# Moving three of the eight largest cache copies from layer 0 to layer 1, in 1 MB pieces on GpSimd's queue, and the delta rule's input loads from the first norm's block to the next one

## The reference

```python
# layer 0: convolution module beside a gated delta rule
z = h @ w_in                                   # 1024 -> 3080 columns
... depthwise convolutions, layer norm, SiLU, l2 norms ...
od, s_new = _gated_delta(q, k, v, g, beta, s0) # recurrent matrices, new state returned
x = x + mixed @ w_out
x = _tail(x, ...)                              # PEER: 8 heads x 16 gathered experts, then a gated embedding
# layer 1: attention with three (window, dilation) groups, then the same kind of tail
outs, caches = _mixer_dilated_sample(h, pos, caches, w_in, w_out)
```

```python
kv_all = jnp.concatenate([cache, kv_new], axis=1)
keep = min(win, L + T)
bufs.append(kv_all[:, L + T - keep:])
```

## Time and profile before

| | |
|---|---|
| time, median of 3 runs | 2553.03 us (2549.06 to 2556.84) |
| profiled execution: its own time | 2553.16 us |
| its span, first to last instruction | 2551.4 us |
| PE busy | 2052.6 us (80%) |
| DVE busy | 1281.3 us (50%) |
| ACT busy | 778.3 us (31%) |
| POOL busy | 644.4 us (25%) |
| moved by DMA | 874.97 MB, mean 343 GB/s |
| mean granted TensorE clock | 0.914 |

### The profile page before, as it was taken

How to read it: one execution, slowest core, us unless ns; L and a number is a source line. 1 busy time by engine, 2 the same in 40 slices (tenths; PEclk the granted TensorE clock), 3 DMA queues, 4 the chain that set the end, 5 groups by cost and what they waited for, 6 DMA issues and landing times. The chain is left out here.

```text
span 2551.4 us, 25632 instructions
## 1 busy us (share of the span) xinstructions
PE 2052.6 (80%) x9026; PEld 1023.6 (40%) x9026; DVE 1281.3 (50%) x3157; ACT 778.3 (31%) x2275; POOL 644.4 (25%) x645
## 2 busy tenths in 40 slices
PE   5975796478887898877689999987887887988766
PEld 4764684253222243322244565454532222432222
DVE  0076653164776667765511031123556677666754
ACT  0143100023444344443411121121234444344443
POOL 0000000024443444434201000000344444454341
PEclk8987775789999999999789999999899999999978
DMA  6794999669999999999938755753899999999995
GB/s 208 265 336 155 330 329 339 246 263 392 427 427 427 427 427 411 427 427 427 421 151 321 273 206 205 286 206 124 326 427 427 427 427 427 427 425 427 427 427 246
DMA packets 129427, 874.97 MB, mean 343 GB/s; under 512 B 15876, under 2 KB 29700, under 8 KB 45195
## 3 DMA queue, kind: packets, MB, share of 16 engines
q0 software_dynamic: 92160, 662.74, 62.5%
q1 hardware_dynamic: 37139, 210.60, 23.3%
HBM read 861.98 MB, written 118.81 MB: 384 GB/s over the span
## 5 line engine op out<-in xcount | busy, mean ns | idle before, releaser
L1433 PE MATMUL tail_acc<-tail_ring,tail_diag 128*128 128x512 f32 x1216 | 596.8, 621 | 113.1 <-ACT tail_diag L1292 111.9
L1180 DVE CUSTOM_DVE_ANT_0 tail_ring<-tail_ring,all_h 128x1024 f32<-128x1024 f32 x344 | 418.7, 1222 | 239.8 <-DMA tail_ring<-in_peer_uv,tail_idx 239.3
L1573 POOL DMA_INDIRECT mid_wring<-in_peer_uv,tail_idx x232 | 239.1, 1031 | 1005.8 <-DVE all_x L1065 528.7
L1433 PE MATMUL tail_acc<-mid_wring,tail_diag 128*128 128x512 f32 x832 | 413.3, 624 | 98.7 <-ACT tail_diag L1292 98.4
L1573 POOL DMA_INDIRECT tail_ring<-in_peer_uv,tail_idx x344 | 368.7, 1072 | 478.6 <-PE tail_acc L1433 412.8
L1433 PEld LDWEIGHTS tail_acc<-tail_ring,tail_diag 128*128 128x128 f32 x1216 | 216.4, 192 | 478.3 <-ACT tail_diag L1292 298.1
L1180 DVE CUSTOM_DVE_ANT_0 mid_wring<-mid_wring,all_h 128x1024 f32<-128x1024 f32 x232 | 283.3, 1223 | 175.0 <-DMA mid_wring<-in_peer_uv,tail_idx 173.5
L1286 ACT ACTIVATE tail_gelus<-tail_dots 128x1 f32<-128x1 f32 x576 | 116.2, 202 | 723.7 <-DVE tail_dots L1180 723.5
L1433 PEld LDWEIGHTS tail_acc<-mid_wring,tail_diag 128*128 128x128 f32 x832 | 147.8, 193 | 352.9 <-ACT tail_diag L1292 223.0
L1684 PE MATMUL mix_acc<-mid_wring,all_hT 128*128 128x512 f32 x576 | 273.2, 609 | 1.5 <-PEq L80 1.4
L1292 ACT ACTIVATE tail_diag<-all_ident,tail_weights 128x128 f32<-128x128 f32 x512 | 205.5, 401 | 26.8 <-PE tail_acc L1433 9.9
(11 more groups left out here) (363 smaller groups left out, 2083.3 us busy)
## 6 DMA issues: line engine op xcount, KB each, us to landing
mid_wring<-in_w_qkv SPq DMA_DIRECT2D x18, 2048.0 KB, 8.5
out_kv_s<-in_cache_kv_w SPq DMA_DIRECT2D x8, 4064.0 KB, 49.5
mix_ring<-in_kT POOLq DMA_DIRECT2D x16, 1024.0 KB
mix_ring<-in_v_rows POOLq DMA_DIRECT2D x16, 1024.0 KB
ab_ring_w<-in_w_in_ab SPq DMA_DIRECT2D x6, 2048.0 KB, 11.1
mix_ring<-in_kT POOLq DMA_DIRECT2D x16, 768.0 KB, 9.2
mix_ring<-in_v_rows POOLq DMA_DIRECT2D x16, 768.0 KB, 9.2
mid_wring<-in_w_out SPq DMA_DIRECT2D x4, 2048.0 KB, 10.5
```

The costliest lines, as they stand in the source:

```text
L1180: V.tensor_tensor_reduce(out=u, in0=u, in1=h[:, g, :], scale=1.0, scalar=0.0, op0=ALU.mult, op1=ALU.add, accum_out=dots[:, n:n + 1]).then_ ...
L1433: last = mm(acc[g][:, c * 512:(c + 1) * 512], diag[:, n % DIAGS, :], v[:, c * 512:(c + 1) * 512], start=first, stop=final)
L1573: pool.indirect_dma_start(slot(r), None, table, bass.IndirectOffsetOnAxis(ap=idx[:, j, i:i + 1], axis=0)).then_inc(landed[r], 16)
```

## The change

Two edits:

1. The loads in `delta_loads` are no longer issued in the first norm's block. They are issued first in the SP stream of the "ab" block (`before`), ahead of the loads of weight chunks 3 to 5.
2. `LATE = 3`: `delta_phase` copies the third cache group for samples 0 to 4 alone. The copies of samples 5 to 7 are cut in pieces of 128 rows (1 MB), 8 pieces a sample, 24 in all. POOL's stream in `dilated_phase` issues one of them behind every load with an odd sl from 5 on, until none is left: behind loads 5, 7, ..., 51. They count on a semaphore of their own, `late_out`, which SP awaits at the end of the kernel.

```diff
-def first_norm_phase(nc, K, T, hT, ahead, later):
+def first_norm_phase(nc, K, T, hT, ahead):
...
                 for to, frm, landed in ahead:
-                    sp.dma_start(to, frm).then_inc(landed, 16)
-                for to, frm, landed in later:
                     sp.dma_start(to, frm).then_inc(landed, 16)
...
-def linear_phase(nc, name, xT, w, width, rows, consume, on="vector", ahead=None, after=None):
+def linear_phase(nc, name, xT, w, width, rows, consume, on="vector", ahead=None, before=(), after=None):
...
             @block.sync
             def _(sp):
+                for to, frm, landed in before:
+                    sp.dma_start(to, frm).then_inc(landed, 16)
                 for c in range(ring if ahead else 0, len(chunks)):
...
-                roll_cache(sp, T, 2, cache_out)
+                roll_cache(sp, T, 2, cache_out, range(DEC_B - LATE))
...
+LATE = 3
...
             @block.gpsimd
             def _(pool):
                 nc.gpsimd.memset(qz[:], 0.0).then_inc(qz_clear, 1)
+                late = roll_pieces(T, 2, range(DEC_B - LATE, DEC_B), 128)
...
                                 pool.dma_start(ring[:, sl % SLOTS_AHEAD, 0:hi - lo], T[name][half, b, :, lo:hi]
                                                ).then_inc(landed[sl % SLOTS_AHEAD], 16)
+                                if sl % 2 and sl >= SLOTS_AHEAD and late:
+                                    to, frm = late.pop(0)
+                                    pool.dma_start(to, frm).then_inc(late_out, 16)
+                assert not late
...
-                first_norm_phase(nc, K, T, hT, W.start, delta_loads)
+                first_norm_phase(nc, K, T, hT, W.start)
...
-                columns_phase(nc, "ab", hT, T["w_in_ab"][0], IN_AB - 8, zT, ahead=W, after=copies)
+                columns_phase(nc, "ab", hT, T["w_in_ab"][0], IN_AB - 8, zT, ahead=W, before=delta_loads, after=copies)
...
-                sp.wait_ge(cache_out, 16 * NG * DEC_B)
+                sp.wait_ge(cache_out, 16 * (NG * DEC_B - LATE))
+                sp.wait_ge(late_out, 16 * len(roll_pieces(T, 2, range(DEC_B - LATE, DEC_B), 128)))
+
+
+def roll_pieces(T, gi, samples, rows):
+
+    src, dst = T[f"cache_kv_w{PATTERNS[gi][0]}"][0], T[f"out_kv{gi}_s"][0]
+    keep = dst.shape[1] - DEC_T
+    drop = src.shape[1] - keep
+    flat = lambda ap: ap.rearrange("r k h e -> r (k h e)")
+    return [(flat(dst[b, r:min(r + rows, keep)]), flat(src[b, drop + r:drop + min(r + rows, keep)]))
+            for b in samples for r in range(0, keep, rows)]
```

More of the change, by code:

```diff
@@ L298, in linear_phase, with columns_phase @@
                 block.scalar(take)
-def columns_phase(nc, name, xT, w, width, outT, ahead=None, after=None):
+def columns_phase(nc, name, xT, w, width, outT, ahead=None, before=(), after=None):
     def consume(eng, c, part, acc):
         return nc.scalar.activation(outT[:, c * 4 + part, :], acc[:, 0:NTOK], ACT.Copy)
-    linear_phase(nc, name, xT, w, width, False, consume, on="scalar", ahead=ahead, after=after)
+    linear_phase(nc, name, xT, w, width, False, consume, on="scalar", ahead=ahead, before=before, after=after)
 def conv_phase(nc, name, K, T, zT, mixT, conv, cache_out):
@@ L1586, with dilated_phase @@
 UNITS = [(j, it) for it in range(2) for j in range(HH)]
-def dilated_phase(nc, K, T, wring, w_in, mixT, w_out_in):
+LATE = 3
+def dilated_phase(nc, K, T, wring, w_in, mixT, w_out_in, late_out):
     hT, h, ident = K["hT"], K["h"], K["ident"]
@@ L2245, in _ @@
                 sp.wait_ge(x_in, 96)
-        cache_out = P.sem("cache_out")
+        cache_out, late_out = P.sem("cache_out"), P.sem("late_out")
         with ExitStack() as c2:
@@ L2267, in build @@
             tail_phase(nc, K, T, 0, wring, [(wring[:, c], T["w_qkv"][:, c], w_in[c]) for c in range(2)])
-            dilated_phase(nc, K, T, wring, w_in, mixT, w_out_in)
+            dilated_phase(nc, K, T, wring, w_in, mixT, w_out_in, late_out)
             tail_phase(nc, K, T, 1, wring, (), w_out_in)
```

## The result

The changed kernel took 2562.93 us (median of 8 runs, 2556.60 to 2567.01) beside 2554.95 us for the kernel before (8 runs, 2549.06 to 2558.11). The ratio is 1.0038, with a 95% interval of 1.0026 to 1.0050: slower by 9.7 us, between 6.6 and 12.8 (the two medians by themselves lie 8.0 apart). Timed again on another chip beside other kernels it was 1.0027 (1.0014 to 1.0040). The sign and the place are as forecast, inside the range; the size is half of the +18.4 us.

What follows compares the result with a forecast made beforehand. Phase ends in layer 0 were taken as bound by SP's transfers, layer 1's bursts by PE with DMA also full. -14.5 - 12.1 + 45 = +18.4 us on 2553.16 gave 2571.5, say 2572; range 2551 to 2593.

Steps and rivals of the forecast that it cites:

- Part 1: First norm's end: with the 14 delta loads moved out, PE starts the projection at about 21.4 us, gaining 14.5 us.
- The 0.8 us of the later chunk 3: Projection: chunk 3's load, queued behind the moved loads, goes some 0.8 us later, hidden under the products of chunks 1 and 2.
- Part 2: Delta rule's end: five copies in place of eight free the state stores, compute is late next; gain 12.1 us.
- Part 3: Layer 1's attention: 15 of 24 pieces delay soon-needed loads in three full bursts, costing 15 us each, 45 in all.
- Price of one: Layer 1's bursts: one 1.049 MB piece takes 3.1 us of all 16 DMA engines, at copies' 337 GB/s.
- my low end: Layer 1's bursts: a piece at the gathers' rate, 2.46 us, with up to 4 us swallowed per burst: 25 us in all.
- my full credit: End of each burst: the four slots' lead swallows up to 4 us of lateness.
- Hidden pieces: First of the rivals, same three bursts: copies overlap loads, 0.2 us left of each piece, 2530 us; chance 0.2.
- Half hidden: Rival, layer 1's bursts: 1.4 to 2.2 us a piece, 21 to 33 us lost, total 2547 to 2559; chance 0.12.
- The stores and the first chunk: Rival, layer 0: either is late all the same, gains 11 and nothing, 2587 us; counted in the forecast's chance.
- Ring order: Loads' queue in layer 1: engines consume a ring in order, so pieces there would hold the loads; no separate size.
- PE's clock: Rival, layer 1's bursts: waiting PE falls to the lower clock, up to 40 us more in one burst, 2590 to 2620; chance 0.06.

Runs made afterwards that it cites:

- runs without pieces: Changed kernel without POOL's 24 copy pieces, three samples of the third cache group not copied, against the kernel before: 0.9909, -23.2 us.
- the fifteen alone: Changed kernel with only the 15 pieces behind the 5th, 7th, 9th, 11th and 13th loads of each burst, against the kernel before: 1.0027.
- tiny pieces: Changed kernel with each of the 24 pieces cut to 8 rows (64 KB), the rest not copied, against the kernel before: 0.9906, -24.0 us.
- half pieces: Changed kernel with each of the 24 pieces cut to 64 of 128 rows (512 KB), against the kernel before: 0.9965, -8.9 us.
- pieces in the gaps: Changed kernel with 4 pieces behind load 19, 16 behind load 35 and 4 behind load 51, against the kernel before: 0.9955, -11.5 us.
- Two placings of 24 pieces in gaps: Changed kernel, against the kernel before: 4, 16, 4 pieces behind loads 19, 35, 51 (0.9955); 4, 8, 4, 8 behind loads 19, 35, 51, 63 (0.9979).
- one sample of eight: Changed kernel with LATE = 1, the last sample's 8 pieces all behind load 35, against the kernel before: 0.9884, 2528.74 us beside 2558.24.

## Why the prediction came out as it did

**Part 1** was right to 0.2 us: 14.7 against 14.5, ended by ACT and not by the first chunk. The 0.8 us of the later chunk 3 did not arise: SP spent 13.4 us on the moved loads at their new place and not the same 18.4 as before, since the first of them took 0.37 us to issue in place of 4.90.

**Part 2** was right in its mechanism: what was late next was compute, as named. In the delta rule's own block the gain was 11.2 us against the 12.1 said. Of the two parts together, 27.3 in the trace against 26.6, 1.4 lie in the blocks between. The runs without pieces give a total of 23 to 24 us. I can't say where those 3 to 4 us are; the trace of the kernel before is a single execution, the tails vary by that much from one to another, and the interval of the run without pieces reaches 26.8.

**Part 3**, the mechanism, was right in each step that could be tried: full bursts, PE held at the slots, 15 of 24 pieces counting (the fifteen alone), bytes and not DMAs (tiny and half pieces), the fourth burst unchanged. **Its price was mis-sized.** The step that failed is "Price of one": 3.1 us a piece, taken from a stretch in which nothing but copies ran, at 337 GB/s. In the bursts loads and copies together moved 400 to 405 GB/s at share 0.98, and the 15 pieces cost 35.3 / 15 = 2.35 us each; the packets say it without a division, 2.46 us in place of 3.14. 1.049 MB at 427 GB/s is 2.46, my low end. By the runs alone it is less, 30 to 33 us over the 15, or 2.0 to 2.2 each. So of the 45 us in the sum 30 to 35 were real, and the gains before it were 23 to 27 and not 26.6.

The same 11.8 us a burst (35.3 / 3) could also have come of my full price with my full credit, 15.6 - 4 = 11.6. The half pieces speak against it: they would then have cost 7.8 - 4 = 3.8 us a burst, 11 in all, and they cost 19.6.

The Trainium skill ("DMA: Bandwidth & Descriptors", section "Anatomy of one DMA — SWDGE (gpsimd) path") takes bytes at 436 GB/s for the moving, an estimate of 2.4 us for 1 MB. It was nearer than my row, and I had set it aside on the strength of that row. With 2.4 the sum would have been about +10. That a share of 1.00 at 337 GB/s is a busy engine and not a fixed rate was the argument of my own first rival ("a busy engine waiting on HBM rather than moving"); it was true by a quarter, not enough to change the sign. What holds copies alone to 337 GB/s I have not tried. The pieces in the gaps, which also ran nearly alone, took 2.8 to 2.9 us a packet.

The landings were 13.7 to 14.0 us at the median with 17.8 at the most, against the 15 to 20 said: the same overstatement.

**The rivals.** Hidden pieces: refuted, with the point at which it decides (1.8 us a piece) passed by 0.5 in the trace and by 0.2 to 0.4 in the runs. Half hidden (1.4 to 2.2 us a piece): the trace's 2.35 and the time of 2562.9 lie above it, the price by the runs at its upper end, so the forecast and this rival meet here. The stores and the first chunk were in time. Ring order, which I had drawn from the same page of the Trainium skill, is not what costs: on SP's queue the loss was the same, 36.2 us. PE's clock: it did fall in places, to 0.91 to 0.94 over a burst, with PE busy 2 to 4 us longer in each of the three, 10 in all. Whether that adds to the loss or only fills time that DMA set anyway is not settled. For the second speak the half pieces, which lost 19.6 us at clock 0.99 to 1.00: twice that is more than the 35.3, so nothing is left over that the clock would have to explain. Against it speaks the burst of values with tiny pieces, which was 3.9 us longer at clock 0.93.

## What to carry to other kernels

A transfer moved out of a full stretch must be costed where it lands, and by three questions: is that stretch full too, which transfer stands behind it soon, and what else, on any queue, has to pass before it is done. A gap in the share of DMA is only as free as the slack of the shortest transfer in it: 4 or 8 pieces in a row were free, 16 held a weight load so that PE stood 13 us, and 8 in the wrong gap held the queue in which four 16 KB moves stood, by 20. And move no more than is late: one sample of eight sufficed here. That three must cost the gain is not shown. Two placings of 24 pieces in gaps kept 5.4 and 11.5 us of it, each time short by one transfer in its way, and one sample's pieces in the bursts were not tried.

## What the runs showed of the hardware

Copies inside HBM moved 337 GB/s at DMA share 1.00 when alone, but mixed with loads to SBUF the total was 400 to 405 at 0.98. A copy's 64 KB packet took 3.14 us alone and 2.46 us in the mixture. Queues did not shield from each other: a 2 MB load on SP's queue took 42 us instead of 8.4 beside 1 MB copies on POOL's, and 24 copies cost the same on either queue. The Trainium skill has each engine take turns between queues packet by packet ("DMA: Bandwidth & Descriptors", "Queues, rings and completion order"). The trace of the run with pieces in gaps agrees: beside 127 packets of 64 KB, SP's queue got 98 of 16 KB and 65 of 512 B through in the same 28 us, so that a queue of small packets fares badly beside one of large ones. A granted clock of 0.91 appeared in a burst where PE was busy 47.5 of 56.4 us; before, at 43.1 of 43.9, it was 1.00, and with half pieces, at 43.6 of 50.1, it was 1.00 too.
